# Queue order of the experts' matrices in a two-block transformer kernel: the first and third matrices of the next quad ahead of the second matrices of this one

## The reference, cut to what matters

```python
def hier_moe(u, w_grp, b_grp, w_exp, b_exp, w1, w3, w2):
    ...
    gate = jax.nn.one_hot(g_sel[:, 0], N_GROUPS, dtype=jnp.float32)[:, :, None] * exp_w[:, None, :]
    out = jnp.zeros_like(t)
    for gi in range(N_GROUPS):
        hid = jax.nn.silu(jnp.einsum('td,edf->tef', t, w1[gi])) * jnp.einsum('td,edf->tef', t, w3[gi])
        hid = hid * gate[:, gi, :, None].astype(hid.dtype)
        out = out + jnp.einsum('tef,efd->td', hid, w2[gi])
    return out.reshape(b, s, d)
```

## Time and profile before

| | |
|---|---|
| median of 3 runs | 1199.23 us (1196.1 to 1200.03) |
| the profiled execution's own time | 1198.67 us |
| span of its trace | 1196.9 us |
| TensorE busy | 1112.2 us (93%) |
| read from HBM | 281.87 MB, mean 237 GB/s over the span |
| stretch of the experts' chunks | 968.14 us to 1184 us |

### The profile page before, as it was taken

How to read it: one execution, slowest core, us unless ns; L and a number is a source line. 1 busy time by engine, 2 the same in 40 slices (tenths; PEclk the granted TensorE clock), 3 DMA queues, 4 the chain that set the end, 5 groups by cost and what they waited for, 6 DMA issues and landing times. The chain is left out here.

```text
span 1196.9 us, 18912 instructions
## 1 busy us (share of the span) xinstructions
PE 1112.2 (93%) x7747; PEld 922.9 (77%) x7747; DVE 715.5 (60%) x1085; ACT 501.8 (42%) x851; POOL 52.9 (4%) x94
## 2 busy tenths in 40 slices
PE   7998899999999999999998999999999999869566
PEld 5886699999789987999997878988887866536333
DVE  4487778778766667778778626745446742212114
ACT  4567544434445645434435425345543422213112
POOL 5000000010000000010000000000000000000000
PEclk9999999999999999999998999999999999979788
DMA  9943368887745343987773652455645799999995
GB/s 275 295 154 105 110 235 278 291 284 274 251 162 190 107 126 115 322 291 267 287 256 97 147 176 71 142 198 174 210 144 211 301 410 410 375 370 372 423 419 206
DMA packets 121904, 285.22 MB, mean 238 GB/s; under 512 B 11709, under 2 KB 72378, under 8 KB 110176
## 3 DMA queue, kind: packets, MB, share of 16 engines
q1 hardware_dynamic: 111904, 249.29, 58.3%
q0 software_dynamic: 9920, 34.80, 8.7%
HBM read 281.87 MB, written 2.20 MB: 237 GB/s over the span
## 5 line engine op out<-in xcount | busy, mean ns | idle before, releaser
L1929 DVE TENSOR_TENSOR w_lo<-ring,w_hi 128x1024 fp32r<-128x1024 f32 (+1 forms) x272 | 319.4, 1211 | 94.2 <-ACT w_hi L1477 84.7
L1477 ACT ACTIVATE w_hi<-ring 128x1024 fp32r<-128x1024 f32 (+1 forms) x272 | 277.7, 1050 | 155.3 <-PE acc L662 130.7
L660 PE MATMUL pp<-x_hi,w_hi 128*128 128x256 f32 x896 | 257.9, 288 | 5.0 <-DVE w_lo L1929 2.9
L662 PE MATMUL pp<-x_hi,w_lo 128*128 128x256 f32 x896 | 254.0, 283 | 0.0
L661 PE MATMUL pp<-x_lo,w_hi 128*128 128x256 f32 x896 | 254.0, 283 | 0.0
L660 PEld LDWEIGHTS pp<-x_hi,w_hi 128*128 128x128 f32 x896 | 172.0, 192 | 12.3 <-issue 7.3
L661 PEld LDWEIGHTS pp<-x_lo,w_hi 128*128 128x128 f32 x896 | 172.2, 192 | 1.4 <-issue 0.2
L662 PEld LDWEIGHTS pp<-x_hi,w_lo 128*128 128x128 f32 x896 | 172.2, 192 | 0.0
L660 PE MATMUL acc<-w_hi,x_hi 128*128 128x512 f32 (+2 forms) x320 | 126.9, 396 | 5.3 <-DVE x_lo L1914 4.1
L662 PE MATMUL acc<-w_hi,x_lo 128*128 128x512 f32 (+2 forms) x320 | 122.7, 383 | 0.0
L661 PE MATMUL acc<-w_lo,x_hi 128*128 128x512 f32 (+2 forms) x320 | 122.5, 383 | 0.0
(11 more groups left out here) (376 smaller groups left out, 1720.1 us busy)
## 6 DMA issues: line engine op xcount, KB each, us to landing
ring<-in_w_up_dram SPq DMA_DIRECT2D x32, 1024.0 KB, 5.6
ring<-in_w_down_dram SPq DMA_DIRECT2D x32, 1024.0 KB, 7.0
exp_ring<-in_w_dram SPq DMA_DIRECT2D x32, 1024.0 KB, 11.7
stage<-in_w_ada_dram POOLq DMA_DIRECT2D x48, 512.0 KB, 6.3
ring<-in_w_in_dram SPq DMA_DIRECT2D x24, 1024.0 KB, 5.4
big<-in_w_dram SPq DMA_DIRECT2D x15, 1024.0 KB, 18.1
ring<-in_w_in_a_dram SPq DMA_DIRECT2D x12, 1024.0 KB, 14.8
mod<-in_w_dram SPq DMA_DIRECT2D x11, 1024.0 KB, 16.3
```

Source lines behind the costliest of these rows:

```text
L660: pe.matmul(out, lhs[0], rhs[0], start=start, stop=False)
L662: return pe.matmul(out, lhs[1], rhs[0], start=False, stop=stop)
L1477: act.activation(shaped(high_half(b, k), raw), raw, ACT.Copy).then_inc(S["hi_ready"], 1)
L1929: dve.tensor_tensor(shaped(low_half(b, k), raw), raw, shaped(high_half(b, k), raw), ALU.subtract).then_inc(S["lo_ready"], 1)
```

## The change: what it does

In the loop the third matrices of quad s+1 now stand directly behind the first matrices of quad s+1, ahead of the wait for `w2_used` and of the second matrices of quad s. Nothing else differs.

```diff
                     sp.wait_ge(S["w1_used"], done)
                     for e in range(4):
                         load_w1(s + 1, e)
+                if s + 1 < QUADS:
+                    sp.wait_ge(S["w3_used"], done)
+                    for e in range(4):
+                        load_w3(s + 1, e)
                 sp.wait_ge(S["w2_used"], done)
                 if s + 1 < QUADS:
                     for e in range(4):
                         load_w2(s, e)
-                    sp.wait_ge(S["w3_used"], done)
-                    for e in range(4):
-                        load_w3(s + 1, e)
```

## The result

| | before | changed |
|---|---|---|
| median | 1199.63 us (1196.1 to 1200.05, 4 runs) | 1222.87 us (1222.39 to 1223.21, 4 runs) |
| span of the profiled execution | 1196.9 us | 1220.6 us |
| ratio | | 1.0193 (95% interval 1.0172 to 1.0215) |

The changed kernel is slower by 1.9%, some 23 us. The forecast was 1223.3 us.

The account below looks back on a forecast made before the run. The prediction took the experts' stretch to be bound by loading; its schedule gave a span of 1219.0 us, plus 2.5 for running early and 1.8 by which time exceeds span: 1223.3 us, range 1214 to 1230.

Parts of the forecast that it names:

- The bound: Experts' stretch: bound by loading, its time being bytes over rate plus the moments in which the queue is empty.
- the schedule: Timeline of load groups and chunks, 9.94 us a group served in order of issue; span 1219.0 us with the change.
- The empty time: Queue empty behind both two-chunk quads and ahead of the last w2: 36.1 us in all, against 11.2 before.
- the 2.5 us: Added because the schedule, replayed on the old order, put the last down part at 1178.0, 2.5 us too early.
- The clock's term: Down parts of chunks 1, 4 and 8, after long waits, take 5.7 us on average instead of 3.62 at full clock.
- The bound of 7.24: Upper bound on a down part run wholly at 1.2 GHz, 7.24 us instead of 5.7; total then 1227.9.
- Issue: Cost of SP being held by a full queue when issuing loads: zero, at most 2 us.
- the faster rival: Early w3 fills the empty queue and later w2 costs nothing, so 11.2 us go: 1187.5 us; chance 3%.
- the order hardly changes: SP is held up issuing w1, or TensorE's existing waits take up the delay: about 1199 us; chance 3%.
- the two neighbours: TensorE keeps its clock or latency is shorter, 1217.0 us, 10%; or clock stays low longer, 1227.9 us, 12%.
- the second neighbour: TensorE's clock stays low longer, into the next up part: 1227.9 us; chance 12%.
- the first of its two consequences: Runs of single-chunk quads: the queue stays full, cost zero, the period stays 3 x 9.94 us.

Follow-up runs that it names:

- The undone passes: Changed kernel with the old order (w2 ahead of w3) in passes s = 1 and s = 3 alone: 1201.12 us, ratio to before 1.0026.
- the run with 10 and 12 added calls: Changed kernel with matmuls added ahead of the w2 wait, 10 calls in quads 1 and 3 and 12 in quad 6: 1223.54 us, ratio 1.0192.
- the run with s = 2 and 4: Kernel before with the new order in passes s = 2 and s = 4 alone: 1190.81 us, ratio 0.9934.
- the second trace of the changed kernel: Changed kernel run again, nothing altered, on the same chip as the second run with added matmuls: 1221.77 us, ratio 1.0192.

## Why the prediction was right

- **The bound** (loading, one queue in the order of issue) held. w2 of quad 1, with w3 of quad 2 ahead of it, released TensorE at 1008.92; the schedule said 1008.3. Later releases, 1053.08, 1082.87, 1125.19, 1155.66 and 1185.53, stood 1.1 to 1.8 us behind the schedule's.
- **The empty time.** Forecast 13.2, 13.2 and 9.7 us, 36.1 in all. The three stretches above lack 12.2, 11.5 and 8.4 us within their bounds, 32.1. With their edges they lack 13.5, 12.7 and 9.5, 35.7 in all:

```profile
1004.00:1023.00 19.00, 14.07 (x168) 6.26 (x169) 4.47 (x9) 2.93 (x4) 0.00 (x0) 0.73 0.32 121
1077.00:1096.00 19.00, 13.13 (x170) 6.28 (x171) 4.56 (x9) 2.93 (x4) 0.00 (x0) 0.76 0.36 139
1180.00:1196.00 16.00, 10.47 (x140) 4.47 (x144) 3.98 (x8) 2.54 (x3) 0.00 (x0) 0.74 0.48 171
```

w1 was issued at 1018.72 and 1091.54, where the schedule had 1017.5 and 1090.3. The undone passes show that this is the cause: where the first two stretches are filled, 20 us are gone.
- **The last down part** at 1204.20; the schedule had 1202.6, and 1205.1 with the 2.5 us by which it ran early on the old order. So that correction was too large by 0.9 us, more than the 0.4 us by which the forecast of the time was off; that it came so near is in part luck. One part of the 2.5 us was there to be read: the last down part begins after a wait of 0.69 us on ACT, in the earlier trace rows and in the changed kernel alike, and the schedule has no such wait. For the rest, w2 of quad 6 released TensorE 1.7 us behind the schedule and the down part behind it was 0.7 us shorter than taken.
- **The clock's term.** The three down parts took 6.27, 5.15 and 5.02 us, 5.5 on average where 5.7 was taken. The bound of 7.24, at 1.2 GHz throughout, was reached in none. That the down part's length sets when the queue fills again is seen for chunk 1 in the run with 10 and 12 added calls, and for chunk 4 in the run with s = 2 and 4. In the second trace of the changed kernel the three took 5.33, 6.21 and 5.40 us, so each single figure is good to about 1 us, and only their sum fits well.
- **Issue.** Zero held. Full queues held SP for some us in a group of loads, but w2 was never late by that.
- **The rivals.** w2 landed 23.65 us after its first load's issue at 985.15 in chunk 1, and 23.2 after 1059.53 in chunk 4, so outstanding transfers did not share in its favour, and the faster rival fell. So did "the order hardly changes". Of the two neighbours, TensorE did not keep its clock (5.0 to 6.3 us for those down parts), and the clock did not stay low into the next up part (6.91 us behind each of the three, as at full clock). The 1227.9 of the second neighbour was moreover the price of whole down parts at 1.2 GHz, with nothing for an up part.
- **What the prediction had wrong in words**, though its schedule had it in numbers: the first of its two consequences, that the new order costs nothing in single-chunk quads. In the passes s = 2 and 4 it gains: with these two alone the kernel is 7.9 us faster than before. The loss of 23 us is therefore a net: the run with s = 1 and 3 undone, with the whole tail loss of 7 to 9 us in it, stands only 3.1 us above before. I had read the faster rival as all or nothing and had not asked pass by pass.

## What to carry to other kernels

On a loading-bound stretch, cost a change of the queue's order by the time in which the queue runs empty: for each group ask what must have landed before the next may be issued, and which group lies behind it as cover. If the next issue has to wait for the use of a group, that group should not be the last in the queue. Waits of the computing engine are a poor guide: here waits of 12 us cost nothing while the queue was full, and the best version keeps waits of 7 to 10 us. They count where an issue hangs on the work behind them, as in chunk 4 of the kernel before. Decide the order place by place: the same swap cost 11 us in one pass and helped in two others, which depends on how many chunks a quad has, so on the data.

## What the runs showed of the hardware that was not expected

The granted clock after a short idle time is not the same each time. In the run with 10 and 12 added calls, TensorE was idle for 2.19 us ahead of the down part both in chunk 1 and in chunk 8; the first took 3.64 us and the second 5.34. So the length of the idle time did not decide it by itself. In chunk 8 the down part began at full clock, after 9.3 us of added matmuls at full clock and the 2.19 us of idle time, and fell to 1.2 GHz within it:

```profile
1187.00:1188.00 1.00, 0.70 (x8) 0.30 (x12) 0.00 (x0) 0.00 (x0) 0.00 (x0) 1.00 0.00 0
1188.00:1189.00 1.00, 1.00 (x12) 0.36 (x8) 0.00 (x0) 0.00 (x0) 0.00 (x0) 0.74 0.00 0
1189.00:1190.00 1.00, 1.00 (x8) 0.23 (x4) 0.14 (x1) 0.00 (x0) 0.00 (x0) 0.50 0.00 0
```

Long waits are not needed for a slow down part: in the run with half of w3 ahead, waits of only 2.85 and 2.64 us ahead of chunks 3 and 6 were followed by down parts of 5.25 and 5.38 us, about as long as those behind waits of 8 to 11 us, while behind waits of 0.8 to 1.5 us every one on the chain that ended last, in any of the traces, took 3.64 to 3.68 us.
